# Attention: query turn, first sums, second decay and next block's products in another order; the value copies and the token scales moved

## The reference

```python
def stick_breaking_attention(q, k, v):
    ...
        z = jnp.einsum('bhqd,bhkd->bhqk', q[:, :, q0:end], k[:, :, :end]).astype(jnp.float32) * scale
        ...
        log_stay = jnp.where(mask, -jax.nn.softplus(z), 0.0)
        stay_after = lax.cumsum(log_stay, axis=3, reverse=True) - log_stay
        log_w = jax.nn.log_sigmoid(z) + stay_after
        w = jnp.where(mask, jnp.exp(log_w), 0.0)
        o = jnp.einsum('bhqk,bhkd->bhqd', w, v[:, :, :end].astype(jnp.float32))
...
def stick_breaking_block(h, k, v, w_q, q_gain, w_o):
    q = rms_norm(heads(h @ w_q), q_gain)
    o = stick_breaking_attention(q, k, v)
    ...
    return o @ w_o
...
    p = jax.nn.softmax(jnp.concatenate([s_win, s_ctx], axis=-1), axis=-1)
...
def pool_mixer(u, w_pool, pool_scale):
    ...
    y = jnp.einsum('bngc,gcd->bngd', pooled, w_pool).reshape(B, N, D_MODEL)
    return y * pool_scale
```

## Time and profile before

| | us |
|---|---|
| median of 3 runs | 1494.72 |
| lowest, highest | 1493.83, 1495.06 |
| the profiled execution | 1494.08 |
| its span, first to last instruction | 1492.2 |
| TensorE busy | 1469.7 (98%) |
| VectorE busy | 1239.9 (83%) |
| ScalarE busy | 826.6 (55%) |
| mean granted TensorE clock, share of full speed | 0.999 |

### The profile page before, as it was taken

How to read it: one execution, slowest core, us unless ns; L and a number is a source line. 1 busy time by engine, 2 the same in 40 slices (tenths; PEclk the granted TensorE clock), 3 DMA queues, 4 the chain that set the end, 5 groups by cost and what they waited for, 6 DMA issues and landing times.

```text
span 1492.2 us, 24944 instructions
## 1 busy us (share of the span) xinstructions
PE 1469.7 (98%) x9630; PEld 1331.9 (89%) x9630; DVE 1239.9 (83%) x1748; ACT 826.6 (55%) x1206; POOL 116.3 (8%) x70
## 2 busy tenths in 40 slices
PE   7999999999999999999999999999999999999998
PEld 7999999999998899999779999987689988999888
DVE  7899898989988869999777987884777898787874
ACT  5554568655446645556765454554656455565452
POOL 0013100001311102111000111100000121000110
PEclk9999999999999999999999999999999999999999
DMA  7667663656675647666233877643235588246660
GB/s 273 250 242 253 239 233 133 224 184 242 233 274 198 226 161 286 235 247 256 85 142 127 297 250 258 254 152 142 95 143 208 203 296 297 108 153 239 233 223 29
DMA packets 44412, 310.32 MB, mean 208 GB/s; under 512 B 5728, under 2 KB 5984, under 8 KB 7200
## 3 DMA queue, kind: packets, MB, share of 16 engines
q1 hardware_dynamic: 42048, 303.33, 55.3%
q0 software_dynamic: 1696, 4.68, 1.1%
q10 hardware_dynamic: 576, 1.05, 0.2%
HBM read 307.93 MB, written 1.05 MB: 207 GB/s over the span
## 4 chain that ended last, share of the span: by engine, by line
PE 94%; DVE 3%; ACT 1%; issue 0%; DMA 0%; SPq 0%; DVEq 0%; ACTq 0%
PE psum L2074 21%; PE psum L1992 13%; PE psum L1999 12%; PE psum L1998 12%; PE psum L2085 11%; PE psum L2164 3%; PE psum L2167 3%; PE psum L2168 3%; PE psum L2295 3%; PE psum L2300 3%; PE psum L2301 3%; DVE w_lo L1124 1%; PE psum L2613 1%; PE psum L2624 1%; PE psum L2543 0%
## 5 line engine op out<-in xcount | busy, mean ns | idle before, releaser
L1124 DVE TENSOR_TENSOR w_lo<-raw,w_hi 128x1024 fp32r<-128x1024 f32 x478 | 590.5, 1253 | 66.8 <-ACT w_hi L551 66.6
L551 ACT ACTIVATE w_hi<-raw 128x1024 fp32r<-128x1024 f32 x478 | 485.4, 1048 | 95.0 <-PE psum L2085 42.1
L2074 PE MATMUL psum<-u,w_hi 128*128 128x512 f32 x1376 | 327.9, 391 | 0.0
L2074 PEld LDWEIGHTS psum<-u,w_hi 128*128 128x128 f32 x1376 | 253.9, 188 | 49.5
L1992 PE MATMUL psum<-u,w_hi 128*128 128x256 f32 (+1 forms) x880 | 255.3, 290 | 11.5 <-DVE u L1221 9.8
L1999 PE MATMUL psum<-u,w_lo 128*128 128x256 f32 (+1 forms) x880 | 249.5, 284 | 0.0
L1998 PE MATMUL psum<-u,w_hi 128*128 128x256 f32 (+1 forms) x880 | 249.5, 284 | 0.0
L1992 PE MATMUL psum<-hid_hi,w_hi 128*128 128x256 f32 x772 | 219.4, 284 | 0.0
L1999 PE MATMUL psum<-hid_hi,w_lo 128*128 128x256 f32 x772 | 218.8, 283 | 0.0
L1998 PE MATMUL psum<-hid_lo,w_hi 128*128 128x256 f32 x772 | 218.8, 283 | 0.0
L2085 PEld LDWEIGHTS psum<-u,w_lo 128*128 128x128 f32 x1376 | 176.5, 191 | 6.7
(11 more groups left out here) (295 smaller groups left out, 1837.4 us busy)
## 6 DMA issues: line engine op xcount, KB each, us to landing
raw<-stream SPq DMA_DIRECT2D x288, 1024.0 KB, 4.8
buf<-tab POOLq DMA_DIRECT2D x2, 768.0 KB, 5.2
x<-x_in SPq DMA_DIRECT2D x2, 512.0 KB, 7.1
buf<-ctx_in POOLq DMA_DIRECT2D x1, 1024.0 KB, 7.1
buf<-poolmat POOLq DMA_DIRECT2D x1, 1024.0 KB, 4.9
out<-x ACTq DMA_DIRECT2D x4, 256.0 KB, 2.4
buf<-late POOLq DMA_DIRECT2D x1, 640.0 KB, 3.9
mod<-mod_row POOLq DMA_DIRECT2D x28, 2.0 KB, 1.9
```

The source lines that it names most:

```text
L551: sc.activation(w_hi[:, u], raw[:, u], ACT.Copy).then_inc(S.hi_ready, 1)
L1124: ve.tensor_tensor(w_lo[:, u], raw[:, u], w_hi[:, u].bitcast(F32), ALU.subtract).then_inc(S.lo_ready, 1)
L2074: ins = te.matmul(bank2(bank), w_hi[:, at + k * P:at + (k + 1) * P], both[:, k, :], start=k == 0, stop=False, skip_group_check=True)
```

## The change

No instruction of a computation is added or dropped; all of it is order. (One split of a weight unit on VectorE, `pump_to(AT["mlp1"] + 4)`, leaves its place, and a later `pump_to(AT["mlp1"] + 5)` catches up on it.)

1. Queries. TensorE: `q_cols` behind half of unit 4 where it stood behind the whole; `turn_queries(0)` behind three quarters of unit 5 where it stood behind half of unit 6; `scores(0)` behind a quarter of unit 6, `scores(1)` behind the rest of it, `scores(2)` and `sums_after(0)` behind half of unit 7, and the last half of unit 7 behind these.
2. ScalarE: `decay_terms(1)` and `weights(0)` ahead of `q_squares(1)`; `decay_terms(2)` cut in two, its ln behind `weights(1)` and `q_roots(1)`. VectorE: `weight_argument(0)`, `softplus(1)` and `mask_scores(3)` ahead of `q_sums(1)`; `q_means(1)` behind `weight_argument(1)`; `attended_lo(1)` ahead of `q_scale(1)`.
3. TensorE: `out_products(1, range(4))` and `sums_after(2)` on the two sides of `turn_queries(1)`, ahead of the wait for the second half of the queries; for that they leave the pass g = 2 of the loop. The new `begins=0` of the products signals no `unit_used` there.
4. Neighbourhood attention: the two value copies of VectorE behind the first two `na_normalise`.
5. Pool mixer: `token_sums` behind `pool_shift(0)` where it stood behind `pool_shift(1)`; ScalarE's root ahead of its copies; the split of unit 4 out of VectorE's way; `pool_tokens(0)` and `(1)` no longer wait for the second copy of the shift rows.

```diff
@@ -901,19 +901,25 @@
                     act.wait_ge(S.cum_ready, g - 2)
                 sc.activation(sp_slots[g % 3], z_slots[g % 4], ACT.Abs).then_inc(S.z_abs, 1)
 
-            def decay_rest(g):
+            def decay_exp(g):
                 d = sp_slots[g % 3]
                 act.wait_ge(S.z_abs, g + 1)
                 sc.activation(d, d, ACT.Exp, scale=-1.0).then_inc(S.e_ready, 1)
+
+            def decay_log(g):
+                d = sp_slots[g % 3]
                 act.wait_ge(S.e_ready, g + 1)
                 sc.activation(d, d, ACT.Ln, bias=1.0).then_inc(S.l_ready, 1)
+
+            def decay_rest(g):
+                decay_exp(g)
+                decay_log(g)
 
             def decay_terms(g):
                 decay_abs(g)
                 decay_rest(g)
 
             decay_terms(0)
-            q_squares(1)
             decay_terms(1)
 
             def weights(g):
@@ -927,10 +933,13 @@
 
 
             weights(0)
+            q_squares(1)
+            attended_hi(0)
+            decay_abs(2)
+            decay_exp(2)
+            weights(1)
             q_roots(1)
-            attended_hi(0)
-            decay_terms(2)
-            weights(1)
+            decay_log(2)
             attended_hi(1)
             q_channels(1)
             decay_terms(3)
@@ -1079,12 +1088,11 @@
                     shift_operand(1)
                 sc.activation(buf[4][:, half(b)], x_t[:, half(b)], ACT.Square).then_inc(S.tok_sq, 1)
             pump_to(AT["mlp1"] + 4)
+            act.wait_ge(S.tok_ms, 1)
+            sc.activation(ty("tok", 2, 2), ty("tok", 0, 2), ACT.Sqrt).then_inc(S.tok_root, 1)
             for h in range(2):
                 act.wait_ge(S.shift_rows, h + 1)
                 sc.activation(buf[1][:, half(h)], psum[:, 2 + h, :], ACT.Copy).then_inc(S.shift_copied, 1)
-                if h == 0:
-                    act.wait_ge(S.tok_ms, 1)
-                    sc.activation(ty("tok", 2, 2), ty("tok", 0, 2), ACT.Sqrt).then_inc(S.tok_root, 1)
             mlp_hi("pool", "H2", 0)
             for b in range(4):
                 if b < 3:
@@ -1661,10 +1669,13 @@
                 dve.wait_ge(S.q_ms, 2 * h + 2)
                 inverse(ty("kh", 16 * h, 16), ty("ky", 16 * h, 16))
 
-            def q_scale(h):
+            def q_inverse(h):
 
                 dve.wait_ge(S.q_root, h + 1)
                 link(inverse_root(ty("na", 16 * h, 16), ty("ky", 16 * h, 16)))
+
+            def q_scale(h):
+
                 for tt in range(2):
                     ve.tensor_tensor(by_heads(q_tok[h][tt]), by_heads(psum[:, 2 * h + tt, :]),
                                      ty("ky", 16 * h + 8 * tt, 8).unsqueeze(2).broadcast_to([P, 8, HD]), ALU.mult)\
@@ -1675,6 +1686,7 @@
             dve.wait_ge(S.q_cols, 1)
             link(ve.tensor_copy(ty("kcol", 2, 2), k_cols[:, 0:2]))
             q_means(0)
+            q_inverse(0)
             q_scale(0)
             pump_to(AT["wo"] + 1)
 
@@ -1718,16 +1730,17 @@
             mask_scores(1)
             softplus(0)
             mask_scores(2)
-            q_sums(1)
             weight_argument(0)
             softplus(1)
+            mask_scores(3)
+            q_sums(1)
+            attended_lo(0)
+            weight_argument(1)
             q_means(1)
-            attended_lo(0)
-            mask_scores(3)
-            weight_argument(1)
+            q_inverse(1)
+            attended_lo(1)
             q_scale(1)
             softplus(2)
-            attended_lo(1)
             pump_to(ATT_LO[0])
             mask_scores(4)
             for g in range(2, NC):
@@ -1853,12 +1866,13 @@
 
             na_scores(0)
             na_scores(1)
-            for kt in range(2, 4):
-                acc_ready("v2", kt)
-                ve.tensor_copy(buf[3][:, half(kt)], psum[:, kt, :]).then_inc(S.acc_read, 2)
             for p in range(8):
                 na_normalise(2 * p)
                 na_normalise(2 * p + 1)
+                if p == 0:
+                    for kt in range(2, 4):
+                        acc_ready("v2", kt)
+                        ve.tensor_copy(buf[3][:, half(kt)], psum[:, kt, :]).then_inc(S.acc_read, 2)
                 if p < 7:
                     na_scores(2 * p + 2)
                     na_scores(2 * p + 3)
@@ -1902,7 +1916,6 @@
             shift_operand(1)
             for b in range(4):
                 add_token_squares(b)
-            pump_to(AT["mlp1"] + 4)
             tok, tok_scale = ty("tok", n=8), ty("tok_scale", n=2)
             dve.wait_ge(S.tok_psum, 1)
             ve.tensor_scalar(tok[:, 0:2], psum[:, 0, 0:4].rearrange("p (q t) -> p q t", t=2)[:, :, 0], 1.0 / D, EPS, ALU.mult, ALU.add)\
@@ -2339,14 +2352,14 @@
             swiglu("ffn2", "ctx", lambda: read("v", 3))
 
 
-            def q_unit(u, kks=(0, 1)):
+            def q_unit(u, kks=(0, 1), tts=(0, 1)):
 
 
                 h, c = u // 4, AT["q"] + u
                 unit_ready(c)
                 for k in (2 * (u % 4) + kk for kk in kks):
                     operand("mix1", k)
-                    for tt in range(2):
+                    for tt in tts:
                         ins = token_product(psum[:, 2 * h + tt, :], c, (k % 2) * 512, k, tt, k == 0, k == NC - 1)
                         if k == NC - 1:
                             ins.then_inc(S.acc_ready, 1)
@@ -2364,16 +2377,18 @@
             for u in range(4):
                 q_unit(u)
             norm_sum("ffn2")
-            q_unit(4)
+            q_unit(4, (0,))
             pe.wait_ge(S.ms_ready, NRM["ffn2"] + 1)
             for tt in range(2):
                 ins = te.matmul(psum[:, 7, KCOL + 2 * tt:KCOL + 2 * tt + 2], eps_ms[:, tt * P:(tt + 1) * P], ident[:, 0:2],
                                 start=tt == 0, stop=True, skip_group_check=True)
             ins.then_inc(S.q_cols, 1)
-            q_unit(5)
-            q_unit(6, (0,))
+            q_unit(4, (1,))
+            q_unit(5, (0,))
+            q_unit(5, (1,), (0,))
             turn_queries(0)
-            q_unit(6, (1,))
+            q_unit(5, (1,), (1,))
+            q_unit(6, (0,), (0,))
             qt_, kt_ = ck(buf[0]), ck(buf[1])
 
             def scores(g):
@@ -2415,36 +2430,43 @@
                                         start=part_ == 0, stop=part_ == 1, skip_group_check=True)
                 ins.then_inc(S.o_ready, 1)
 
-            def out_products(k, blocks):
+            def out_products(k, blocks, begins=None):
                 c = AT["wo"] + k
                 unit_ready(c)
                 for n in blocks:
                     ins = product(bank2(n // 2)[:, n % 2, :], c, n * P, u_hi[:, k, 0:T], u_lo(k),
-                                  k == 0 and n % 2 == 0, k == NC - 1)
+                                  k == 0 and n % 2 == 0, k == NC - 1, begins=begins)
                     if k == NC - 1 and n % 2:
                         ins.then_inc(S.acc_ready, 1)
 
             scores(0)
+            q_unit(6, (0,), (1,))
+            q_unit(6, (1,))
+            scores(1)
             q_unit(7, (0,))
-            scores(1)
-            q_unit(7, (1,))
             scores(2)
             sums_after(0)
+            q_unit(7, (1,))
             scores(3)
             attend(0)
             sums_after(1)
             out_products(0, range(4))
             attend(1)
+            operand("att", 1)
+            out_products(1, range(4), 0)
             turn_queries(1)
+            sums_after(2)
             pe.wait_ge(S.q_out, 4)
             out_products(0, range(4, NC))
             scores(4)
             for g in range(2, NC):
-                sums_after(g)
+                if g > 2:
+                    sums_after(g)
                 if g + 3 < NC:
                     scores(g + 3)
                 ahead = 4 if g + 3 < NC else 6
-                out_products(g - 1, range(ahead))
+                if g > 2:
+                    out_products(g - 1, range(ahead))
                 attend(g)
                 out_products(g - 1, range(ahead, NC))
             operand("att", NC - 1)
@@ -2715,12 +2737,13 @@
                 pool_channels(g)
             pe.wait_ge(S.pool_shift_lo, 1)
             pool_shift(0)
+            token_sums()
             pool_shift(1)
-            token_sums()
             pool_shift(2)
             pool_shift(3)
-            pe.wait_ge(S.shift_copied, 2)
             for g in range(3):
+                if g == 2:
+                    pe.wait_ge(S.shift_copied, 2)
                 pool_tokens(g)
             begun[0] = AT["pool"] + 1
             sqrelu("mlp1", "pool", lambda: pool_tokens(3))
```

## The result

The changed kernel takes 1497.72 us (median of 22 runs, 1494.84 to 1498.93) against 1494.53 for the kernel before on the same chip (22 runs, 1493.83 to 1495.40). The ratio is 1.0018, with a 95% interval of 1.0012 to 1.0024: 2.7 us slower by it, 3.2 by the medians. The forecast was 1495.4, range 1493.0 to 1497.6. The median stands 0.1 above its end; carried over by the ratio to the 1494.72 of the kernel before on which the forecast was built, it is 1497.4, just inside.

| mean granted clock of the run | runs | time, us |
|---|---|---|
| 1.000 | 6 of 22 | 1494.84 to 1495.88 |
| 0.999 and 0.998 | 7 of 22 | 1496.85 to 1498.01 |
| 0.997 | 9 of 22 | 1497.82 to 1498.93 |

The account below looks back on a forecast made before the run. TensorE, busy 98% of the span, was taken as the bound, so only its waits count. Attention +1.5, value copies -0.45 and pool mixer -0.4 give +0.65 on the median of 1494.72: 1495.4 us, range 1493.0 to 1497.6.

Parts of the forecast that it names:

- The order's price: Attention up to attend(2): attend(0) 1.5 us earlier, then 3.0 us more from there to attend(2); together +1.5 us.
- (a): TensorE at the third product of sums_after(1), for attended_lo(0) behind mask_scores(3) and q_sums(1): new wait of 0.4 us.
- (b): TensorE before attend(1), for sums, weight argument and weights as before: kept wait of 0.6 us.
- (c): TensorE before out_products(1), for attended_lo(1): new wait of 1.1 us, in place of 1.2 for q_out.
- (d): TensorE before scores(5), right behind scores(4), for the two score banks: new wait of 1.1 us.
- (e): TensorE before attend(2), right behind scores(5), for mask, softplus, weight argument and weights: new wait of 1.8 us.
- The sum: Whole kernel: attention +1.5, value copies -0.45, pool mixer -0.4, together +0.65 us.
- The value copies: Neighbourhood attention: first transpose no longer waits with the copies behind na_normalise; -0.45 us (0 to -0.5).
- The pool mixer: Pool mixer: pool_tokens(0) starts earlier, held only by scale_z(0); -0.4 us (0 to -0.7).
- later pairs wait too: Attention behind attend(2): each of five attends waits some 0.5 us more; +2.5 on top, 1497.9 us; chance 0.06.
- The clock: Rival: idle TensorE falls to half clock; 10 us at 1.2 instead of 2.4 GHz adds 5, 1500 us; chance 0.01.

Follow-up runs that it names:

- experiment 10: Changed kernel with only weight_argument(2) moved ahead of mask_scores(4) on VectorE: 1495.44 us against 1494.71 for the kernel before, ratio 1.0010.
- 12: The changed kernel itself, run again on chip 6: 1498.22 us against 1494.71 for the kernel before, ratio 1.0022.
- experiment 11: Kernel of experiment 8 with attended_lo(0) ahead of q_sums(1) and attended_hi(0) ahead of q_squares(1): 1495.06 us against 1494.71 before, ratio 1.0000.
- experiment 5: Changed kernel with zero-tile filler matmuls, 5 before the sixth pair's scores and 6 before attend(2): 1495.79 us against 1494.87 before, ratio 1.0007.
- experiment 8: Changed kernel with weight_argument(2) ahead of mask_scores(4), second half of out_products(1) between the fifth and sixth pairs' scores: 1494.27 us against 1494.87 before.
- 7: Changed kernel with 6 zero-tile filler matmuls before attend(2) only: 1495.95 us against 1494.87 for the kernel before, ratio 1.0007.
- experiment 2: Kernel before with only half of out_products(1) and sums_after(2) put ahead of the wait for the turned queries: 1498.65 us against 1494.98, ratio 1.0027.
- 3: Changed kernel with the move of half of out_products(1) and sums_after(2) undone: 1497.41 us against 1494.98 for the kernel before, ratio 1.0017.
- 9: Kernel of experiment 3 with zero-tile filler matmuls, 8 before the second query turn and 3 behind it: 1495.55 us against 1494.71 before, ratio 1.0006.
- experiment 1: Changed kernel with zero-tile filler matmuls, 9 before the sixth pair's scores and 14 before attend(2): 1498.41 us against 1494.98 before, ratio 1.0024.

## Why the prediction came out as it did

- **The order's price held.** +1.63 at `attend(2)` for +1.5. Its halves: `attend(0)` 1.28 earlier (1.5 forecast) and +2.91 from there to `attend(2)` (3.0). The waits (a) to (e) were forecast, counted from start to start, at 0.4, 0.6, 1.1, 1.1 and 1.8; the rows show 0.29, 0.56, 1.01, 1.15 and 1.65 of idle time, for the releasers named. The wait (d) for the two banks of the scores was paid in full. The third L2429 came at 751.56, within the 751.2 to 751.6 given. This sum needed the clock to hold, and up to here it did.
- **The sum held** for the runs at full clock: +1.63 - 0.46 - 0.2 = +1.0 where I had +0.65, and 1494.84 to 1495.88 us where I had 1495.4.
- **The value copies held**: 0.46 for 0.45, in the changed kernel and alone.
- **The pool mixer was mis-sized**: 0.2 for 0.4. I put the start of the first `scale_z` at 1298.5 in the time of before; it came at 1302.74 - 4.08 = 1298.66, behind a copy that ended 0.1 later than I had it (1302.63 - 4.08 = 1298.55 for 1298.45) and a handover. The mechanism was right: L1933 is what `pool_tokens(0)` waits for.
- **The later pairs** didn't wait more; the rival "later pairs wait too" is not what happened, though the time is near its 1497.9: no wait stands between `attend(2)` and the last `attend`. That the median came out at the end of the range is luck. The upper part of the range was made of longer waits, which didn't come; the fall that did was left out of it.
- **The clock is the step that failed.** Its fall was put at nothing in the sum and at a chance of 0.01, on two grounds: "the granted clock is full throughout, the 9.5 us wait included", and "the new waits are shorter than that". The first is wrong, and the second carries nothing. The windows of before do read 1.00 in the first 16 us:

```profile
4.00:8.00 4.00, 0.00 (x0) 1.00 0.95 339
8.00:12.00 4.00, 2.47 (x11) 1.00 1.04 429
```

but the matmuls behind the wait read otherwise (the kernel before, timeline of TensorE):

```profile
9.88 0.41 PE L1998 MATMUL psum<-u,w_hi 128*128 128x256 f32 x1
10.10 0.41 PE L1999 MATMUL psum<-u,w_lo 128*128 128x256 f32 x1
...
12.94 0.28 PE L1998 MATMUL psum<-u,w_hi 128*128 128x256 f32 x1
13.06 0.28 PE L1999 MATMUL psum<-u,w_lo 128*128 128x256 f32 x1
```

0.41 us at a spacing of 0.21 is what the same instructions show in the changed kernel at a granted clock of 0.50, and 0.28 at 0.12 is full clock. So TensorE began at half clock, and the column did not show it at the start of the program. The longest wait was no proof of a clock that holds: half clock is what stood behind it. The Trainium skill, "TensorE: Matmul & The Clock Gate", section "What's actually happening", says that half clock is the state of an idle TensorE; these rows agree with it, and so do the changed kernel's 750 to 758.

Nor must a shorter wait be harmless if a longer one is. On one chip, TensorE passed an idle 1.01 us behind 0.55 us at full clock (the traces of experiments 10 and 12) and fell behind 0.74 and 1.01 (experiment 11). The same page of the Trainium skill, section "A second HAM failure mode: psum-queue depth-cycling", tells of a kernel whose short idle times between groups of matmuls come often enough to move the clock down and up. The changed kernel agrees as far as it goes: its clock fell with no wait above 1.65 us, though once and not in a cycle. The price was put at 5 us for 10 us at half clock; it was 2.75 for 7. The chance was far too small: 16 of 22 runs.

What stays open is which pattern of idle time brings the clock down. The longer waits between 739 and 753 us, in order of time, and the runs that were slowed, told by time and clock together (the mean clock alone does not tell: six of the 11 runs of experiment 5 read 0.999 and lost nothing). The changed kernel's 22 runs were on a chip that the record doesn't name:

| kernel | chip | idle, us | slowed |
|---|---|---|---|
| before | all | 0.56, 0.92 | none seen |
| 8 | 11 | 0.56, 1.01, then 0.51 | 0 of 11 |
| 7 | 11 | 0.56, 1.01, then 1.15 | 0 of 11 |
| 10 | 6 | 0.55, 1.01, then 1.15, 0.91 | 5 of 11 |
| 11 | 6 | 0.74, 1.01, then 0.36 | 6 of 11 |
| 2 | 13 | 0.55, 1.28, then 1.15, 1.66 | 5 of 8 |
| changed | not named, 6 | 0.56, 1.01, then 1.15, 1.65 | 16 of 22, 10 of 11 |
| 3 | 13 | 0.56, 2.21, 0.92 | 11 of 11 |

It is a list of what ran, not a rule: the eleventh falls behind less idle time than the seventh bears, on another chip, so that chip and pattern can't be told apart there. Why some runs of one kernel fall and others don't is in no trace.

## What to carry to other kernels

Price a new wait of a full TensorE twice: its own length, and what the clock takes if it lies beside other waits. Here two waits of 2.8 us in all, 0.9 us of work apart, cost as much again behind them in the profiled run. Where a wait can't be closed, moving independent products into it (experiment 8) or even work without use that fits it (experiments 5 and 9) went with full clock in all runs; a filler that is too long costs its excess in full (experiment 1). When one kernel's runs fall into groups, read the clock of each run before the medians.

## What the runs showed of the hardware

- The granted clock column can read 1.00 where the durations are those of half clock: the first 2.7 us of matmuls in the trace of the kernel before, the first 4.0 us in the changed kernel's, up to 5.7 us in others (experiment 11). Compare durations of one form, 0.28 against 0.41 us here, before building on the column.
- This first stretch differs from trace to trace, and what follows is moved with it: the mark at the last sum of squares, ahead of all that was changed, stands at 715.22 after 2.7 us at half clock (experiment 1) and at 716.39 after 5.5 us (experiment 10). So a part of the 1 to 2 us by which runs of one kernel differ may come from here (not shown for runs without a trace), and steps are best counted from a mark.
- The fall came within the second wait in the changed kernel (0.85 for 750 to 751) and some 0.5 us behind the wait in the eleventh, amid matmuls. Once half clock was on, it lasted some 7 us in the first and some 3 us in the second.
- One and the same kernel fell in some runs and not in others, on chip 13 (experiment 2) and on chip 6 (experiments 10 to 12).
- A matmul by a 128x128 float32 tile, 128 columns long, is two records and takes 0.25 us here (18 records in 2.27 us in experiment 1).
